# Two heads of a pair in one attention step of 256 queries each, with their value products on the two column halves of TensorE

## The reference

```
def stick_breaking(q, k, v, q_pos, k_pos, bias):
    z = einsum('bqhd,bkhd->bhqk', q, k) * DH_A ** -0.5 + bias[None, :, None, None]
    mask = k_pos[None, :] < q_pos[:, None]
    log_beta = log_sigmoid(z)
    log_keep = where(mask, log_sigmoid(-z), 0.0)
    later = cumsum(log_keep, axis=3, reverse=True) - log_keep
    att = where(mask, exp(log_beta + later), 0.0)
    return einsum('bhqk,bkhd->bqhd', att, v)
```

## Time and profile before

| | |
|---|---|
| median of 3 runs | 3787.16 us (3779.07 to 3790.33) |
| span of the profiled execution | 3774.0 us |
| between that span and the median | 13.2 us |
| stage with the attention, from its first score product | 536 to 1278 us |
| mean granted TensorE clock of the span | 0.957 |

### The profile page before, as it was taken

One profiled execution on the slowest core, in us unless ns is written; L12 is line 12 of the kernel. 1 busy time (PEld: TensorE's weight loads), 2 busy tenths in 40 slices (PEclk: granted clock), 3 DMA queues, 4 the chain that ended last, 5 costly groups with the idle time before them and its releaser, 6 DMA issues. The chain is left out here.

```text
span 3774.0 us, 53101 instructions
## 1 busy us (share of the span) xinstructions
PE 3470.4 (92%) x20032; PEld 3115.9 (83%) x20032; DVE 1756.1 (47%) x3346; ACT 1189.0 (32%) x2192; POOL 303.9 (8%) x796
## 2 busy tenths in 40 slices
PE   7999786999999889999999989988888999999997
PEld 7999674666666679999999978987677999999996
DVE  6444324566656444334334465324644434433436
ACT  5433233455445433111211144112444211111113
POOL 0000113223323000000000000001200000000000
PEclk9999888999999989999999989998988999999998
DMA  4323551222111121111111111223521111111111
GB/s 138 101 101 106 169 166 41 67 49 74 34 35 35 34 82 40 45 39 39 50 40 43 44 29 59 87 71 137 173 60 28 45 44 40 44 44 39 39 50 47
DMA packets 311047, 246.37 MB, mean 65 GB/s; under 512 B 78165, under 2 KB 273049, under 8 KB 310900
## 3 DMA queue, kind: packets, MB, share of 16 engines
q1 hardware_dynamic: 299080, 201.56, 18.2%
q0 software_dynamic: 11824, 42.93, 3.1%
HBM read 185.83 MB, written 58.62 MB: 65 GB/s over the span
## 5 line engine op out<-in xcount | busy, mean ns | idle before, releaser
L449 PE MATMUL ffn_ps<-ffn_in_hi,ffn_w_hi 128*128 128x368 f32 x2112 | 703.4, 333 | 34.6 <-DVE ffn_w_lo L892 22.0
L450 PE MATMUL ffn_ps<-ffn_in_lo,ffn_w_hi 128*128 128x368 f32 x2112 | 701.6, 332 | 0.0
L451 PE MATMUL ffn_ps<-ffn_in_hi,ffn_w_lo 128*128 128x368 f32 x2112 | 700.1, 331 | 0.0
L449 PEld LDWEIGHTS ffn_ps<-ffn_in_hi,ffn_w_hi 128*128 128x128 f32 x2112 | 400.1, 189 | 41.2 <-DVE ffn_w_lo L892 23.1
L450 PEld LDWEIGHTS ffn_ps<-ffn_in_lo,ffn_w_hi 128*128 128x128 f32 x2112 | 399.9, 189 | 0.5
L451 PEld LDWEIGHTS ffn_ps<-ffn_in_hi,ffn_w_lo 128*128 128x128 f32 x2112 | 399.9, 189 | 0.0
L449 PE MATMUL ffn_ps<-ffn_h_hi,ffn_w_hi 128*128 128x368 f32 x1056 | 353.8, 335 | 10.8 <-DVE mix L965 9.9
L451 PE MATMUL ffn_ps<-ffn_h_hi,ffn_w_lo 128*128 128x368 f32 x1056 | 348.9, 330 | 0.0
L450 PE MATMUL ffn_ps<-ffn_h_lo,ffn_w_hi 128*128 128x368 f32 x1056 | 348.1, 330 | 0.0
L965 DVE TENSOR_TENSOR mix<-ffn_ps,mix 128x368 f32<-128x368 f32 x480 | 256.2, 540 | 191.1 <-PE ffn_ps L451 190.4
L836 ACT ACTIVATE ffn_w_hi<-ffn_w_raw 128x1024 fp32r<-128x1024 f32 x132 | 136.1, 1045 | 463.1 <-PE ffn_ps L451 463.1
(11 more groups left out here) (497 smaller groups left out, 6586.3 us busy)
## 6 DMA issues: line engine op xcount, KB each, us to landing
ffn_w_raw<-in_w_ffn_gate_dram SPq DMA_DIRECT2D x44, 512.0 KB, 3.8
ffn_w_raw<-in_w_ffn_up_dram SPq DMA_DIRECT2D x44, 512.0 KB, 3.8
ffn_w_raw<-in_w_ffn_down_dram SPq DMA_DIRECT2D x44, 512.0 KB, 3.7
first_w_raw<-in_w_in_ab_dram SPq DMA_DIRECT2D x27, 512.0 KB, 4.0
rwkv_prep<-xT POOLq DMA_DIRECT2D x4, 2208.0 KB, 7.4
qkv_proj<-qk_out_sb POOLq DMA_DIRECT2D x16, 552.0 KB, 3.0
atts_k_page<-in_cache_k_dram SPq DMA_DIRECT2D x32, 256.0 KB, 3.1
atts_v_page<-in_cache_v_dram SPq DMA_DIRECT2D x32, 256.0 KB, 2.9
```

Of the source, the lines that this page charges most:

```text
L449: pe.matmul(out, w_hi, x_hi, start=first, stop=False)
L450: pe.matmul(out, w_hi, x_lo, start=False, stop=False)
L451: return pe.matmul(out, w_lo, x_hi, start=False, stop=last)
```

## The change

A step now takes both heads of a pair, with 256 queries each, instead of one head with 512. The blocks are four of 256 queries (9, 7, 5 and 3 key tiles) and one of the 16 meta queries: 25 steps in a pair, 100 in all, of which 20 in a pair have 2 x 256 columns, four 2 x 128, one 2 x 16. The columns of a pair come to 11296 in both kernels. What each part issues in a step:

- `scores`: one product per head (and one mask product per head on the diagonal), each of 256 columns; `sums` and `rest`: one product over both heads, 512 columns, from a pattern of two rows;
- ScalarE: the scaling copy once per head, since the bias is the head's; all else once for both heads, as before; VectorE: once for both heads, and one copy out of all 128 partitions;
- `values`: one product per head, to partitions 0 to 63 and then 64 to 127 of the same bank, directly one behind the other.

Keys and values are loaded for both heads in two parts, for the queries and keys above position 528 and for those below, with the reloading waits moved to match.

```diff
-    G = 512
+    G = 256
     steps = []
-    blocks = [(N_META + G, 8), (N_META, 4)]
+    q_blocks = [(N_META + G * b, 2 * b + 2) for b in (3, 2, 1, 0)]
     for i in range(NPAIR):
-        for hh in range(2):
-            for q0, top in blocks:
...
+        for q0, top in q_blocks:
+            for kt in range(top, -1, -1):
+                lo = max(0, N_META + P * (kt - 1) - q0) if kt else 0
+                steps.append((i, q0, G, kt, lo, kt > 0 and N_META + P * (kt - 1) >= q0, kt == 0))
+        steps.append((i, 0, N_META, 0, 0, True, True))
...
+                    if part == 0 and n == 0 and 0 < i < NPAIR:
+                        sp.wait_ge(z_mm, t)
+                        part_waits(sp, parted)
+                        load_k(i, 1)
...
-                if n % HEAD_STEPS == 0:
-                    pe.wait_ge(k_loaded[hh], (i + 1) * 16)
+                    pe.wait_ge(k_loaded[0], (i + 1) * 32)
+                    part_waits(pe, parted)
+                if n % PAIR_STEPS == q_blocks[0][1] - LOW_TOP:
+                    pe.wait_ge(k_loaded[1], (i + 1) * 32)
                     part_waits(pe, parted)
                 if n:
-                    pe.wait_ge(z_scaled, n)
+                    pe.wait_ge(z_scaled, 2 * n)
...
-                mm = pe.matmul(att[0:keys, Z, lo:width], k_in[:, hh, k0:k0 + keys],
-                               q_in[:, i % 2, q0 + lo:q0 + width], start=True, stop=not diag, skip_group_check=True)
...
+                for hh in range(2):
+                    mm = pe.matmul(att[0:keys, Z, hh, lo:width], k_in[:, hh, k0:k0 + keys],
+                                   q_in[:, i % 2, q0 + lo:q0 + width], start=True, stop=not diag, skip_group_check=True)
...
-                pe.matmul(att[pair(hh), O, lo:width], v_in[0:keys, kt, hh, :],
-                          w[0:keys, n % 2, lo:width], start=first[n], stop=last, skip_group_check=True
-                          ).then_inc(pv_mm, 1)
+                for hh in range(2):
+                    mm = pe.matmul(att[pair(hh), O, 0, lo:width], v_in[0:keys, kt, hh, :],
+                                   w[0:keys, n % 2, hh, lo:width], start=first[n], stop=last, skip_group_check=True)
+                mm.then_inc(pv_mm, 1)
...
-                        act.activation(zs[0:keys, t % 3, lo:width], att[0:keys, Z, lo:width], ACT.Identity,
-                                       scale=DH ** -0.5, bias=bias8[0:keys, head:head + 1]).then_inc(z_scaled, 1)
+                        for hh in range(2):
+                            head = 2 * steps[t][0] + hh
+                            act.activation(zs[0:keys, t % 3, hh, lo:width], att[0:keys, Z, hh, lo:width], ACT.Identity,
+                                           scale=DH ** -0.5, bias=bias8[0:keys, head:head + 1]).then_inc(z_scaled, 1)
```

More of the change, by code:

```diff
@@ L2176, in shape @@
         def shape(n):
-            i, hh, q0, width, kt, lo, diag, last = steps[n]
+            i, q0, width, kt, lo, diag, last = steps[n]
             keys = P if kt else N_META
@@ L2641, in attention_steps @@
                         scores(t)
-                    if part == 1 and 0 <= t - 3 < NS and not steps[t - 3][7]:
+                    if part == 1 and 0 <= t - 3 < NS and not steps[t - 3][6]:
                         rest(t - 3)
@@ L2721, in attention_steps @@
                         keys, lo, width, k0 = shape(t)
-                        head = 2 * steps[t][0] + steps[t][1]
                         act.wait_ge(z_mm, t + 1)
@@ L2737, in attention_steps @@
                         keys, lo, width, k0 = shape(n)
-                        x = w[0:keys, n % 2, lo:width]
+                        x = w[0:keys, n % 2, :, lo:width]
                         act.wait_ge(w_done, n + 1)
@@ L2908, in attention_steps @@
                 for t, part in s_steps:
-                    if part == 0 and 0 <= t - 5 < NS and steps[t - 5][7]:
+                    if part == 0 and 0 <= t - 5 < NS and steps[t - 5][6]:
                         n = t - 5
-                        i, hh, q0, width, kt, lo, diag, last = steps[n]
+                        i, q0, width, kt, lo, diag, last = steps[n]
                         dve.wait_ge(pv_mm, n + 1)
-                        dve.tensor_copy(mix[pair(hh), i, q0:q0 + width], att[pair(hh), O, 0:width]).then_inc(out_done, 1)
+                        dve.tensor_copy(mix[:, i, q0:q0 + width], att[:, O, 0, 0:width]).then_inc(out_done, 1)
                     n = t - 2
```

109 lines of the change are left out of this document (60 added, 49 removed).

## The result

The changed kernel takes 3774.11 us (median of 20 runs, 3762.45 to 3784.50), the kernel before, on the same chip, 3783.28 us (20 runs, 3771.49 to 3799.13). The ratio is 0.9971, with a 95% interval of 0.9963 to 0.9980: some 11 us faster (8 to 14), where 31 were forecast. The direction came as forecast and the value products shrank as forecast; the size did not come.

What follows compares the result with a forecast made beforehand. TensorE was taken to bound the stage's later part, with attention as filler in its queue. Value products 39, fewer steps +3, score products -1, waits -10 gave 31 us: 3787.2 to 3756 us, range 3738 to 3776 for 8 times in 10.

Steps and rivals of the forecast that it cites:

- The value products: TensorE's value products: two heads overlap in column halves, 0.66 us a step; 40.6 us gained, 39 us counted.
- the rule of the Trainium skill: Products start and end strictly in program order; by it the value products would gain about 22 us and not 39.
- Fewer steps: 20 steps go, and with them TensorE's turns for `sums` and `rest`: 3 us gain, bounds nothing to 10 us.
- More score products and ScalarE's copies: 80 more score products, loads hidden: 1 us lost, 10 if not; ScalarE's copies 21 us more, covered, not counted separately.
- the upper ends named: Largest losses: 10 us if score products' weight loads weren't hidden, up to 21 us if ScalarE's copies weren't covered.
- Waits that come up: Shorter value products let the recurrence's latency show on TensorE: 10 us lost, bounds nothing to 20 us.
- Loads: Key and value loads land in time: nothing counted; 17 us at each of three pair changes if one fell behind.
- The clock: TensorE's granted clock in the stage's later part was expected at 0.95 to 0.97; no term in the sum.
- The fourth rival: TensorE's clock falls and the kernel is slower: 6.4 us per 0.01, 31 us gone at 0.91; chance 4%.
- The plan: Places the recurrence's items by the number of attention parts gone by; the prediction had no term for it.
- The base: Whole kernel before: profiled span 3774.0 us plus 13.2 us to the median, 3787.2 us, from which the gain was taken.

Runs made afterwards that it cites:

- same_half_even: Changed kernel with both heads' value products in column half 0 (no overlap) and the recurrence's items placed by attention columns, not steps: 3781.5 us, ratio 0.9999 to the kernel before.
- before_split: Kernel before, with score product and ScalarE's scaling copy of each step wider than 128 columns cut in two halves, 96 more of each: 3793.9 us, ratio 1.0024.
- same_half: Changed kernel with both heads' value products sent to column half 0, so that they can't overlap: 3791.5 us, ratio 1.0023 to the kernel before.
- even_plan: Changed kernel with the recurrence's items placed by attention columns gone by, not by steps: 3757.6 us, ratio 0.9926 to the kernel before.
- before_warm: Kernel before, with 93 extra products of 128 columns and 64 rows ahead of waits in the tile's chain: 3806.3 us, ratio 1.0062.
- warm_chain2: Changed kernel with 102 extra products of 128 columns ahead of waits in the tile's chain, added to the bank's unused half: 3766.1 us, ratio 0.9943 to the kernel before.

## Why the prediction was wrong

- *The value products* were sized right: 37.8 us less against 40.6 forecast (39 in the sum), one step 0.65 us against 0.66. That the halves take their products independently of the queue's order, read from two places in the trace, was right, and the trace was right against the rule of the Trainium skill ("TensorE: Matmul & The Clock Gate", Part 3).
- *Fewer steps*: forecast 3 us. same_half_even has the new steps and the split, and stands at the time of the kernel before; the split costs 8 us by before_split, so the fewer steps gain about 8, by subtraction of two runs and not by a run of their own. The busy time of `sums` and `rest` (L2631, L2633, L2640, L2642) shows where; it falls by 13 us, from 172.9 to 159.6. Two of the four groups, before and after:

```profile
L2610 PE MATMUL attp_ps<-mixers_keep_hi,mixers_neg_tri 128*128 128x512 f32 (+5 forms) x120 | 51.0, 425 | 4.0 <-DVE mixers_keep_lo L2922 3.6 <-issue 0.2
L2619 PE MATMUL attp_ps<-mixers_keep_hi,mixers_neg_rest 128*128 128x128 f32 (+2 forms) x96 | 46.0, 479 | 0.4 <-DVE mixers_w L2943 0.4
```

```profile
L2631 PE MATMUL attp_ps<-mixers_keep_hi,mixers_neg_tri 128*128 128x512 f32 (+3 forms) x100 | 48.7, 487 | 0.6 <-DVE mixers_keep_lo L2947 0.6
L2640 PE MATMUL attp_ps<-mixers_keep_hi,mixers_neg_rest 128*128 128x512 f32 (+1 forms) x80 | 40.0, 499 | 0.3 <-DVE mixers_w L2968 0.3
```

- *More score products and ScalarE's copies*: forecast 1 us and nothing. 96 of each cost 9 us in the kernel before, so 80 some 8. That was within the upper ends named, 10 and 21 us, but the value taken was at the wrong end. A copy took 470 ns at 256 columns, as read from the earlier trace rows, but two of them one behind the other overlap, which the prediction's 2 x 473 - 687 left out:

```profile
L2751 ACT ACTIVATE mixers_zs<-attp_ps,mixers_bias 128x256 f32<-128x256 f32 x128 | 53.6, 470 | 124.0 <-PE attp_ps L2616 89.2 <-PE attp_ps L2619 30.6 <-DVE mixers_w L2968 4.0
```

128 copies keep ScalarE busy for 53.6 us and not for 60.2, and all copies grow from 68.8 to 78.4 us, 10 and not 21 us more. ScalarE's total in the stage is even 354.6 against 356.7, because 20 steps of its other instructions went.
- *Waits that come up*: forecast 10 us; idle time in the stage is 14.6 us longer, of which the overlap brings 7 (same_half to the changed kernel). The prediction laid all of it on the shorter value products; half of it came with the new steps and their places.
- *Loads*: forecast nothing, and right. From 608 to 1278 us no product waits for a DMA; the one wait for keys, before that, is 5.4 us against 5.7.
- *The clock* is the step that failed. The forecast took 0.95 to 0.97 for the stage's later part; it was 0.90. The fourth rival had named the way and the price: 6.4 us for 0.01, all of the 31 us gone at 0.91. It got 4%, and only as a way to be slower, so the sum has no term for the clock at all. The only reason given was that TensorE would still be busy in nearly nine tenths. What happened lies between: the kernel stayed faster and lost 21 us by the mean clocks. In the profiled pair, 0.96 to 0.90, the rival's price gives 38 us, and the span after is indeed 2 us longer and not 31 shorter. The argument against the rival was true and didn't help: TensorE is busy in 0.90 of these 670 us, and the clock fell all the same, near the ends of pairs. It was an average over a stage, which the prediction's first paragraph warns of.
- *The plan* was shown in the order of instructions, but nothing was counted on it. The prediction had looked for which attention part stands where, not for how much work each place holds. even_plan shows 17 us for that, and with it the kernel takes 3757.6 us, near the 3756 that the sum gave. That is luck in part: fewer steps and the split measured 8 and 8 us and not 3 and 1, and its clock is still 0.002 below that of the kernel before.
- *The base*: the 13.2 us between span and median were for the most part the difference between a fast execution and typical ones, not time outside the span; in the run after, the two are 1.8 us apart. The median of before is 3783.3 us in 20 runs, not 3787.2, so 4 us of the forecast's time come from there and none of its 31 us.

The balance against the kernel before, by the runs: value products -38, of which the overlap gives back 13 by the clock and 7 by waits (same_half to the changed kernel); score products and copies +8; fewer steps -8; plan by steps, with no overlap, +9. That is -9, where the ratio gives -11, with an uncertainty of some 4 us in each term. It is no check: split, steps and plan add up to same_half's +9 by the way they were found. What stays open is how the clock's fall in one place is set off by the work in it; the runs show only that the same instructions in another spacing keep it up.

## What to carry to other kernels

Where work is taken from TensorE, look in short windows, not over the stage, for the places that will become thin, and put a price on the clock there as a term of the sum, not as a rival. When steps are merged or cut, a plan that counts steps must be looked at again: count the work that each of its places holds. A filler product paid here only where the clock had fallen, and not always there; measure it against the same filler, of the same shape, in the kernel before.

## What the runs showed of the hardware

- Value products of two heads in the two column halves run side by side, also when each half has several in its queue: eight passes of 256 columns take 1.08 us, as four in a single half do.
- Runs of the changed kernel differ in granted clock, 0.945 to 0.951, and in time with it, by 29 us for 0.01 over the whole kernel. Two profiled executions can therefore hide a difference of 10 us that 20 runs show.
- TensorE was busy in 0.90 of 670 us after the change and in 0.92 before, and its granted clock there was 0.90 and 0.96: a stage's busy share didn't tell its clock. (At the lower clock a product is busy for longer: L2521 took 0.70 us instead of 0.49.)
- Two ScalarE copies of 256 columns one behind the other overlap: 128 of 470 ns each keep the engine busy for 53.6 us.
- A filler of 64 rows and 128 columns held up the next product for 0.42 us, one of 128 rows for 0.33 us (before_warm, warm_chain2).
- TensorE came back at 1.2 GHz after 14.9 us without work (2.05 us for eight passes), and at nearly full speed after 2.1 us (1.13 us), when 24 us of fillers lay before.
